# All products of constants taken out of TensorE's stream in a two-block transformer kernel

## The chip, the cores and the metric

The kernel runs on one core of a Trainium2 chip. The metric is the device time of one execution in microseconds (us); lower is better. All times below are from runs on the chip.

## What is computed

The input is a latent sequence of 512 tokens and a context of 256 tokens, both of width 1024, in fp32. Two blocks follow one another.

```python
for layer in range(DEPTH):                       # 2
    sh1, sc1, g1, sh2, sc2, g2 = ada_mod(c[:, None, :], ada_w[layer], ada_b[layer])
    h_lat = rmsnorm(x_lat, norm_mix[layer]) * (1 + sc1) + sh1
    h_ctx = rmsnorm(x_ctx, norm_mix[layer]) * (1 + csc1) + csh1
    if layer % 2 == 0:
        y_ctx, y_lat = hyena_mlstm_mixer(h_ctx, h_lat, ...)
    else:
        y_ctx, y_lat = mla_mixer(h_ctx, h_lat, not last, ...)
    x_lat = x_lat + g1 * y_lat
    x_lat = x_lat + g2 * conv_ffn(rmsnorm(x_lat, norm_ffn[layer]) * (1 + sc2) + sh2, *ffn_p[layer])
...
h = rmsnorm_2(x, norm_mix_w[l])                  # second block, 1 layer
attn = gqa_attention(...)
ssd = bidirectional_ssd(...)
x = x + merged @ w_out[l]
x = x + hierarchical_moe(rmsnorm_2(x, norm_ffn_w[l]), ...)   # 16 experts, 2 per token
```

None of the outputs depends on the products that this document is about.

## The kernel before, in words

The program is a row of stages, each a block in which every engine has its own instruction stream. Streams wait for one another by semaphores. At a block's end stands a barrier for all engines (line 169 in the profile): the next stage begins on every engine when the last one has come to its end. So what a stage costs is set by its slowest engine, and what comes first in a stage can't start before that.

Most of the work is `three_passes` (lines 303 to 305): each fp32 operand is cut into a high and a low part, and TensorE takes three products of them. Weights come by `Stream` (lines 240 to 283): SyncE's queue loads a tile, ScalarE rounds it to the high part (`high`, line 278), VectorE subtracts for the low part (`low`, line 282), and TensorE waits for `ready`. A second load into the same place waits for `low`. At a stage's start TensorE waits for the first tile, unless an earlier stage has fetched it.

Norms have a serial part. In `Norm` ScalarE squares (line 379), VectorE adds the tiles (388), `sum_and_spread` on TensorE sums over partitions (400), ScalarE takes the root (414), VectorE the reciprocal (431) and a diagonal (435), TensorE spreads it (406), and VectorE and ScalarE scale, shift and split tile by tile (441, 421, 425, 448), and TensorE begins its projection with the first tile. `NormOfNorm` (lines 534 to 627) is the same for two norms in one, with 569 and 577 on TensorE. The latent attention's inner norms (lines 640 to 713) have 656 and 663 there.

`keep_running` (lines 286 to 289) issues n products on TensorE of an identity and the constants: 128x128 by 128x256, fp32. They wait for nothing, read tensors that never change, and write a PSUM bank that nobody reads. An fp32 product is two passes in the profile. It stands at 25 places in the source, 37 runs in the executed stream:

- at the start of a stage that waits for weights, 8 products: projections, residual projections, attention inputs (lines 1009, 1341, 1610, 1701, 2413, 2771)
- around the norms: 16 or 20 ahead of the sum, 2 or 6 behind it, 4 or 6 behind the spread (394 to 408, 565 to 579), and 12, 3 and 12 in the latent attention's norms (650 to 666)
- in the recurrent stage (mLSTM): 2, 6 and 3 (1915, 1954, 1960)
- in the state-space stage: 8 ahead of `spread_rows`, 10 ahead of the first unit's product (line 2943), 1 ahead of each of the next five, 16 at the end (2926, 2938, 2963)
- in the router of the experts: 8, 8 and 16 (3440, 3449, 3454)

TensorE's stream is executed in order, so a product of constants delays every real one behind it if that one could already run. The state-space stage on TensorE, where the prediction has a term of its own: `spread_rows(u)` (2903 to 2905) makes a unit's exponents, ScalarE takes the exponential (3010), VectorE multiplies (3081, 3085), and TensorE's 2943 waits for that (`prob`); unit u + 2 is spread ahead of unit u's product. VectorE's `grow` (3046) comes ahead of its first 3081.

## Time and profile before

| | |
|---|---|
| median of 3 runs | 3084.03 us (3082.63 to 3085.0) |
| the profiled execution's own time | 3083.98 us |
| its span, first to last instruction | 3082.2 us |
| busy: TensorE, its weight loads | 2844.0 us, 2309.2 us |
| busy: VectorE, ScalarE, GpSimd | 1721.4 us, 1218.5 us, 181.2 us |
| moved by DMA | 359.71 MB, mean 117 GB/s |

In the profile TensorE is PE (its weight loads PEld), VectorE DVE, ScalarE ACT, GpSimd POOL, SyncE SP. L289 is line 289 of the kernel before. The clock (PEclk) is the share of TensorE's full clock of 2.4 GHz that was granted; it has two levels, 1.00 and 0.50 (1.2 GHz), and a value between them is a mean over a stretch. "idle before" is the time in which the engine had nothing to do just ahead of the instruction, and "<-" names what ended it.

### The profile page before, as it was taken

Reading aid. Unit: us, or ns where it says so; the run is one execution under the profiler, and the core shown is the slowest. Engines: PE = TensorE matmul, PEld = TensorE weight load, DVE = VectorE, ACT = ScalarE, POOL = GpSimd, SP = SyncE. Lnnn points to the kernel's source line nnn. Section 1 sums busy time; section 2 is a strip of 40 time slices with the busy share of each in tenths; the row PEclk is TensorE's granted clock in tenths of the full one; section 3 lists DMA queues with packets and bytes.
Section 4 is the critical chain, followed back from the end, with each engine's and each line's share of the span. In section 5 each row is a group of like instructions: output and inputs, shape, how many; then the busy total and the mean of one; then the engine's idle time right before and its main releaser. Section 6 shows DMA issues by size and latency. Waiting matters only on the chain. (4 is left out here: it accounts for less than half of the span.)

```text
span 3082.2 us, 37662 instructions
## 1 busy us (share of the span) xinstructions
PE 2844.0 (92%) x14114; PEld 2309.2 (75%) x14114; DVE 1721.4 (56%) x2450; ACT 1218.5 (40%) x1621; POOL 181.2 (6%) x160
## 2 busy tenths in 40 slices
PE   7899989799999989998999999989979989899998
PEld 3764877688888888786887887867746667777776
DVE  3764643635767443535854433352258564788887
ACT  4210322324233242433534343244426422577776
POOL 0000001100011000000000000000000000122221
PEclk9989999899999999999999999999988998999999
DMA  5500320021345243202012221312200024799996
GB/s 234 176 21 14 123 96 2 28 93 61 121 141 180 74 150 97 67 25 68 1 49 89 97 95 70 99 55 89 89 8 1 1 70 165 272 364 356 354 356 220
DMA packets 79468, 359.71 MB, mean 117 GB/s; under 512 B 13554, under 2 KB 18451, under 8 KB 54772
## 3 DMA queue, kind: packets, MB, share of 16 engines
q1 hardware_dynamic: 61204, 307.74, 27.9%
q0 software_dynamic: 18144, 50.36, 5.4%
q8 instruction: 76, 1.25, 0.2%
q14 instruction: 44, 0.36, 0.0%
HBM read 356.47 MB, written 16.25 MB: 121 GB/s over the span
## 5 line engine op out<-in xcount | busy, mean ns | idle before, releaser
L303 PE MATMUL ps<-rounded,rounded 128*128 128x512 f32 (+1 forms) x3540 | 1301.8, 368 | 117.9 <-DVEq L1090 20.1
L304 PE MATMUL ps<-rounded,rounded 128*128 128x512 f32 (+1 forms) x3540 | 1281.8, 362 | 0.0
L305 PE MATMUL ps<-rounded,rounded 128*128 128x512 f32 (+1 forms) x3540 | 1280.1, 362 | 0.0
L303 PEld LDWEIGHTS ps<-rounded,rounded 128*128 128x128 f32 x3540 | 677.4, 191 | 240.0 <-issue 76.1
L305 PEld LDWEIGHTS ps<-rounded,rounded 128*128 128x128 f32 x3540 | 676.5, 191 | 102.8
L304 PEld LDWEIGHTS ps<-rounded,rounded 128*128 128x128 f32 x3540 | 678.0, 192 | 96.1
L282 DVE TENSOR_TENSOR rounded<-work,rounded 128x1024 fp32r<-128x1024 f32 (+3 forms) x224 | 306.2, 1369 | 745.0 <-ACT rounded L278 744.7
L278 ACT CAST rounded<-work 128x1024 fp32r<-128x1024 f32 (+3 forms) x224 | 260.5, 1165 | 711.7 <-PE ps L305 614.8
L3716 DVE TENSOR_TENSOR rounded<-work,rounded 128x2048 fp32r<-128x2048 f32 x138 | 309.8, 2285 | 71.6 <-ACT rounded L3536 71.6
L3536 ACT CAST rounded<-work 128x2048 fp32r<-128x2048 f32 x138 | 258.9, 1912 | 74.7 <-PE ps L305 74.7
L289 PE MATMUL ps<-cst 128*128 128x256 f32 x562 | 151.6, 429 | 35.9 <-PEq L169 35.9
L289 PEld LDWEIGHTS ps<-cst 128*128 128x128 f32 x562 | 120.1, 219 | 62.3 <-issue 43.1
L278 ACT ACT_TABLE_LOAD x34 | 43.6, 1283 | 192.4 <-PE ps L305 183.9
L493 DVE SCALAR_TENSOR_TENSOR work<-work,silu_c 128x256 f32<-128x256 f32 x224 | 103.6, 483 | 13.3 <-DMA work<-in_ada_w 7.4
L2283 PE MATMUL ps<-rounded,rounded 128*128 128x256 f32 (+2 forms) x416 | 96.5, 372 | 5.6 <-PEq L169 5.1
L1173 ACT ACTIVATE work<-work 128x768 f32<-128x768 f32 (+1 forms) x44 | 32.5, 739 | 125.3 <-DVE work L1208 125.3
L3414 POOL DMA_INDIRECT out_x<-h,whole x23 | 60.1, 2613 | 349.9 <-ACT h L3578 335.2
L1086 DVE SCALAR_TENSOR_TENSOR work<-ps,vec,work 128x255 f32<-128x255 f32 (+3 forms) x116 | 72.4, 653 | 14.5 <-ACT work L1056 10.6
L2283 PEld LDWEIGHTS ps<-rounded,rounded 128*128 128x128 f32 (+1 forms) x416 | 65.2, 196 | 19.0 <-issue 8.4
L2333 ACT CAST rounded<-ps 128x768 fp32r<-128x768 f32 (+1 forms) x64 | 44.4, 694 | 69.3 <-PE ps L2309 69.2
L1486 PE MATMUL ps<-work 128*128 128x512 f32 x160 | 71.5, 606 | 0.0
L918 DVE SCALAR_TENSOR_TENSOR work<-work,silu_c 128x512 f32<-128x512 f32 x98 | 67.7, 745 | 5.9 <-DMA work<-in_ada_w 4.2
(509 smaller groups left out, 2493.5 us busy)
## 6 DMA issues: line engine op xcount, KB each, us to landing
work<-in_moe SPq DMA_DIRECT2D x138, 1024.0 KB, 8.2
work<-in_ffn_up SPq DMA_DIRECT2D x44, 1024.0 KB, 4.8
work<-in_ada_w POOLq DMA_DIRECT2D x80, 512.0 KB, 4.1
work<-in_ffn_down SPq DMA_DIRECT2D x66, 512.0 KB, 3.4
work<-in_ada_w SPq DMA_DIRECT2D x4, 2048.0 KB, 27.2
work<-in_w_out SPq DMA_DIRECT2D x16, 512.0 KB, 3.5
work<-in_w_gates SPq DMA_DIRECT2D x16, 512.0 KB, 3.5
work<-in_w_in_hy SPq DMA_DIRECT2D x12, 512.0 KB, 4.7
```

What stands on the lines that cost most here:

```text
L278: self.k.nc.scalar.copy(self.parts[s][0], self.raw[s]).then_inc(self.rounded[s], 1)
L282: self.k.nc.vector.tensor_tensor(self.parts[s][1], self.raw[s], self.high_plain[s], ALU.subtract).then_inc(self.ready[s], 1)
L289: k.nc.tensor.matmul(k.bank(bank, 2 * P), k.const("ident"), k.cst[:, 0:2 * P], start=True, stop=True)
L303: k.nc.tensor.matmul(out, sh, mh, start=start, stop=False, **more)
L304: k.nc.tensor.matmul(out, sh, ml, start=False, stop=False, **more)
L305: return k.nc.tensor.matmul(out, sl, mh, start=False, stop=stop, **more)
L493: done = self.k.nc.vector.scalar_tensor_tensor(out=total, in0=tile, scalar=by, in1=total, op0=ALU.mult, op1=ALU.add)
L1086: nc.vector.scalar_tensor_tensor(out=out, in0=k.pair(p)[:, lo + o:hi + o], scalar=k.col(conv_w, n + tiles * (o + taps // 2)), in1=out, op0 ...
L1486: last = nc.tensor.matmul(bank(group, part), tab[part][:, a, n * P:(n + 1) * P], src[:, a, :], start=a == 0, stop=a == count - 1)
L2283: last = nc.tensor.matmul(scores(u)[:, t0 - lo:t0 - lo + n], queries, keys, start=i == 0, stop=i == len(products) - 1)
L3536: nc.scalar.copy(ring.parts[:, c % ring.SPLIT, 0, :], ring.raw[c % ring.RAW]).then_inc(ring.rounded, 1)
L3716: V.tensor_tensor(ring.parts[:, s, 1, :], ring.raw[c % ring.RAW], ring.plain[:, s, 0, :], ALU.subtract).then_inc(ring.ready, 1)
```

## The change

`keep_running` is deleted, with every call of it. Where a norm's `begun` branch or an `elif` held only such a call, the branch goes or is left with its `return`. Nothing else is touched.

```diff
-def keep_running(k, n=8, bank=7):
-
-    for _ in range(n):
-        k.nc.tensor.matmul(k.bank(bank, 2 * P), k.const("ident"), k.cst[:, 0:2 * P], start=True, stop=True)
...
     def sum_and_spread(self, pe):
         k = self.k
         if self.begun:
-            keep_running(k, 6, self.spare)
             return
-        keep_running(k, 16, self.spare)
         pe.wait_ge(self.added, DT - 1)
...
         last.then_inc(self.summed, 1)
-        keep_running(k, 2, self.spare)
         for a in range(self.n):
...
-        keep_running(k, 6, self.spare)
...
         @block.tensor
         def _(pe):
-            keep_running(k, 12, 6)
             done = 0
...
                 last.then_inc(summed, 1)
-            keep_running(k, 3, 6)
...
                 last.then_inc(spread_done, 1)
-            keep_running(k, 12, 6)
...
             if norm:
                 norm.sum_and_spread(pe)
-            elif not stream.ahead:
-                keep_running(k)
...
-            keep_running(k, 8)
             pe.wait_ge(rows_high, 1)
             pe.wait_ge(rows_ready, 1)
             pe.wait_ge(masked, 5)
...
                     widen(u // 2)
-                if u < 6:
-                    keep_running(k, 1 if u else 10)
                 pe.wait_ge(prob, u + 1)
...
             last.then_inc(sum_done, 1)
-            keep_running(k, 16, 2)
```

The other calls go in the same way.

What this does to TensorE's stream is seen at the start of the state-space stage's units, TensorE before (the last exponent row turned, then the first units; "waits" are semaphores):

```order
L289 MATMUL ps<-cst 128x256 x8
L2903 MATMUL ps<-rounded_41984_14620,rounded_50560_14618 128x512 [waits even_33,even_7,even_6]
L2905 MATMUL ps<-rounded_50304_14616,rounded_50560_14618 128x512
L2911 MATMUL ps<-rounded_41984_14620,rounded_38400_14619 128x512
L2912 MATMUL ps<-rounded_42496_14621,rounded_38400_14619 128x512
L289 MATMUL ps<-cst 128x256 x10
L2943 MATMUL ps<-work,h 64x128 [waits even_8,even_12]
L2943 MATMUL ps<-work,h 64x128 x3
L2903 MATMUL ps<-rounded_41984_14620,rounded_50560_14618 128x512 [waits even_11]
L2904 MATMUL ps<-rounded_42496_14621,rounded_50560_14618 128x512
L2905 MATMUL ps<-rounded_50432_14617,rounded_50560_14618 128x512
L289 MATMUL ps<-cst 128x256
```

And the same stretch of the changed kernel, whose line numbers are smaller (L2903 is L2875, L2943 is L2912):

```order
L2868 MATMUL ps<-cst,row 16x128 x3
L2875 MATMUL ps<-rounded_41984_14410,rounded_50560_14408 128x512 [waits even_33,even_7,even_6]
L2877 MATMUL ps<-rounded_50304_14406,rounded_50560_14408 128x512
L2883 MATMUL ps<-rounded_41984_14410,rounded_38400_14409 128x512
L2884 MATMUL ps<-rounded_42496_14411,rounded_38400_14409 128x512
L2912 MATMUL ps<-work,h 64x128 [waits even_8,even_12]
L2912 MATMUL ps<-work,h 64x128 x3
L2875 MATMUL ps<-rounded_41984_14410,rounded_50560_14408 128x512 [waits even_11]
L2876 MATMUL ps<-rounded_42496_14411,rounded_50560_14408 128x512
L2877 MATMUL ps<-rounded_50432_14407,rounded_50560_14408 128x512
```

The runs of L289 are gone, and every wait stands at the instruction where it stood.

## Rows read from the trace of the kernel before

**Rows 1.** The page, part 1: busy time, share of the span, instructions
```profile
PE 2844.0 (92%) x14114; PEld 2309.2 (75%) x14114; DVE 1721.4 (56%) x2450; ACT 1218.5 (40%) x1621; POOL 181.2 (6%) x160
```

**Rows 2.** The page, part 5, products of constants: busy us, mean ns, idle before
```profile
L289 PE MATMUL ps<-cst 128*128 128x256 f32 x562 | 151.6, 429 | 35.9 <-PEq L169 35.9
```

**Rows 3.** Windows behind bare gaps: stretch, length, PE busy (count), PEclk, DMA share, GB/s
```profile
93.55:103.55 10.00, 10.00 (x47) 0.77 0.54 174
...
490.95:500.95 10.00, 10.00 (x50) 0.84 0.01 2
...
2488.20:2498.20 10.00, 10.00 (x31) 0.69 0.32 107
2541.41:2551.41 10.00, 10.00 (x35) 0.79 0.30 105
```

**Rows 4.** Timeline of TensorE: start, us, what, idle before; shortest of those gaps
```profile
490.95 0.40 PE L303 MATMUL ps<-rounded,rounded 128*16 128x256 f32 x1 [3.54 <-DVE rounded L2106]
```

**Rows 5.** Windows behind products of constants, same columns
```profile
607.34:617.34 10.00, 10.00 (x63) 1.00 0.35 105
...
1592.82:1602.82 10.00, 10.00 (x37) 0.83 0.34 106
...
2274.62:2284.62 10.00, 10.00 (x83) 1.00 0.01 2
```

**Rows 6.** Windows of one stage at either clock, TensorE, same columns
```profile
2068.61:2074.50 5.89, 5.89 (x14) 0.50 0.55 178
2076.00:2081.89 5.89, 5.89 (x27) 1.00 0.21 58
```

**Rows 7.** Timeline of TensorE in the norms
```profile
684.89 2.40 PE L400 MATMUL ps<-cst,row 128*128 128x1 f32 x12 [1.84 <-DVE row L388]
...
689.72 2.93 PE L406 MATMUL ps<-h,cst 128*128 128x128 f32 x12 [0.51 <-DVE h L435]
...
1293.33 1.40 PE L400 MATMUL ps<-cst,row 128*128 128x1 f32 x12
...
1295.63 1.60 PE L406 MATMUL ps<-h,cst 128*128 128x128 f32 x12
...
1360.08 2.29 PE L656 MATMUL ps<-cst,h 128*128 128x1 f32 x20
...
1363.61 2.39 PE L663 MATMUL ps<-h,cst 128*128 128x128 f32 x20
...
2047.62 1.95 PE L577 MATMUL ps<-h,cst 128*128 128x128 f32 x16
```

**Rows 8.** Timeline of VectorE in the norm at 1354 to 1373
```profile
1357.98 0.96 DVE L695 TENSOR_TENSOR h<-h 128x768 f32<-128x768 f32 x1 [0.50 <-ACT h L672]
...
1365.08 3.91 DVE L707 SCALAR_TENSOR_TENSOR work<-work,vec,ps 128x512 f32<-128x512 f32 x5
```

**Rows 9.** Timeline of TensorE, the next wait behind the restart at 2052.64
```profile
2068.61 0.79 PE L303 MATMUL ps<-rounded,rounded 128*128 128x512 f32 x1 [4.65 <-DVE rounded L282]
```

**Rows 10.** Timeline of the state-space stage, TensorE and VectorE
```profile
2407.31 0.68 DVE L3058 TENSOR_TENSOR rounded<-ps,rounded 16x512 fp32r<-16x512 f32 x1 [0.84 <-ACT rounded L2991]
...
2411.27 0.49 PE L2903 MATMUL ps<-rounded,rounded 16*128 16x512 f32 x1
...
2413.76 2.98 DVE L3081 TENSOR_TENSOR work<-work 128x512 f32<-128x512 f32 x1 [1.37 <-ACT work L3010]
...
2420.69 1.28 DVE L3081 TENSOR_TENSOR work<-work 128x512 f32<-128x512 f32 x2
2421.65 1.09 PE L2943 MATMUL ps<-work,h 128*64 128x128 f32 x8
...
2423.67 0.59 PE L289 MATMUL ps<-cst 128*128 128x256 f32 x2
```

**Rows 11.** Timeline, work that covers other runs of the products
```profile
2608.85 2.48 DVE L3610 SCALAR_TENSOR_TENSOR h<-h,work 128x1024 f32<-128x1024 f32 x2
...
88.82 1.04 ACT L278 CAST rounded<-work 128x1024 fp32r<-128x1024 f32 x1 [8.48 <-DMA work<-in_w_in_hy]
```

More of the change, by code:

```diff
@@ L564, in sum_and_spread @@
         k = self.k
-        keep_running(k, 20, self.spare)
         pe.wait_ge(self.added, 2 * DT - 2)
@@ L571, in sum_and_spread @@
         last.then_inc(self.summed, 1)
-        keep_running(k, 6, self.spare)
         for n, (spread, diagonal) in enumerate(((self.spread, self.diagonal), (self.first_spread, self.first_diagonal))):
@@ L578, in sum_and_spread @@
                                    start=True, stop=True).then_inc(self.spread_done, 1)
-        keep_running(k, 4, self.spare)
     def shift(self, act):
@@ L1339, in _ @@
         def _(pe):
-            if not stream.ahead:
-                keep_running(k)
             with pe.Fori(0, turns) as i:
@@ L1608, in _ @@
                 norm.sum_and_spread(pe)
-            elif not stream.ahead:
-                keep_running(k)
             def turn(i, first):
@@ L1700, in _ @@
         def _(pe):
-            keep_running(k)
             for j, a in enumerate(token_tiles):
@@ L1914, in _ @@
                 prepare(g)
-            keep_running(k, 2, 2)
             pe.wait_ge(topped, 2)
@@ L1952, in carry @@
                         last.then_inc(state, 1)
-            keep_running(k, 6, 2)
             pe.wait_ge(masked, 3)
@@ L1959, in _ @@
             weigh(0)
-            keep_running(k, 3, 2)
             pe.wait_ge(fade_high, 1)
@@ L2412, in _ @@
         def _(pe):
-            keep_running(k)
             with pe.Fori(0, turns) as i:
@@ L2770, in _ @@
         def _(pe):
-            keep_running(k)
             for j in range(4):
@@ L3439, in _ @@
             pe.wait_ge(tok_kept[0], 4)
-            keep_running(k, 8, 4)
             pe.wait_ge(chosen, 1)
@@ L3448, in _ @@
             last.then_inc(summed, 1)
-            keep_running(k, 8, 4)
             pe.wait_ge(matched, 1)
@@ L3453, in _ @@
             last.then_inc(listed, 1)
-            keep_running(k, 16, 4)
             def turn_seen(t, half):
```

## The prediction, made before the changed kernel was run

> **What bounds the kernel now.** I read the page first: TensorE is busy for 92% of the span [rows 1], so the question at each place is what keeps the other 8%, and what speed TensorE has. The products of constants are 562 passes (281 products, two passes each) with 151.6 us of busy time, and next to them TensorE has 35.9 us of idle time that ends in its own queue, at the barrier between stages [rows 2]. That is 4.9% of the span, but it isn't 4.9% on the path: at most places these products stand in time in which TensorE would wait for something else. So I went through the timeline run by run, in 37 runs, and asked two things of each: did the next real matmul come later than what it waits for, and at which clock did it run.
>
> The clock is the second half. The windows view gives the granted clock in the first 10 us after a restart. Nine restarts come after at least 3.5 us of idle TensorE with no product of constants in the gap; the shortest gap is 3.54 us [rows 4]. All nine run at first at the low level (1.2 GHz): the mean clock over the 10 us is between 0.69 and 0.84, 0.77 over the nine [rows 3]. A clock of 0.77 over 10 us is 2 x 0.23 x 10 = 4.6 us at half speed; the ends are 3.2 and 6.2 us. Twelve restarts come right behind products of constants: nine have 1.00 (2.4 GHz), the first and the last of them shown, and three have 0.83, so 3.4 us at the low level in spite of the products [rows 5]. What low time costs is read in one stage: 14 matmuls pass in 5.89 us at 0.50, 27 at 1.00 [rows 6]; a microsecond at the low level loses 1 - 14/27 = 0.48 us wherever TensorE is the bound.
>
> **The change, part by part.** It removes all 281 products, adds nothing, and moves nothing; no wait, queue or DMA changes.
>
> *Restarts that are fast now.* After the change the stretches ahead of 607.34, 696.98, 1301.57, 1376.35, 1389.26, 1412.04, 1656.48, 2052.64 and 2274.62 are gaps without work on TensorE of 4.3 us or more; ahead of 1656.48 and 2052.64 it is 3.1 us, with only 2 us of passes between that gap and a longer one. By [rows 3, 4] each restarts at the low level for 4.6 us, 4.6 x 0.48 = 2.2 us. Behind eight of them TensorE works almost without a break to the end of its stage, and the barrier there waits for the last matmul's eviction, so the loss is on the path: 8 x 2.2 = 17.6 us. Behind 2052.64 it isn't: TensorE next waits 4.65 us for VectorE [rows 9], which in this stretch works through its own queue, and the loss goes into that wait. Nothing there.
>
> *Restarts that are slow now* (325.37, 452.88, 1592.82): 3.4 us become 4.6, 3 x 1.2 x 0.48 = 1.8 us. The ones at 2488 and 2633 are slow now for as long as any; nothing.
>
> *The norms.* There few small fp32 products are a link of a serial chain. The norm at 684.89 runs at the low level now, the one at 1293 at full speed: L400's twelve passes take 2.40 against 1.40 us, L406's twelve 2.93 against 1.60 [rows 7]. After the change all are slow.
> - At 1293: L406 is waited for by VectorE, 1.3 us more. L400 loses 1.0, but could start 0.9 us earlier; 0.
> - At 1360: L656 waits for VectorE's L695, which ends at 1358.94 [rows 8], and starts at 1360.08, since 12 products of constants stand ahead of it: 1.1 us are given back. Its twenty passes then take 4.0 instead of 2.29, and L663's twenty 4.9 instead of 2.39 [rows 7]. The first part of L663 is hidden by VectorE's L701; the fourth of the five L707 [rows 8] waits for the second part, which ends at about 1368.9 instead of 1366.0, while VectorE would be there at 1367.1. 1.9 us in all.
> - At 2043: sixteen passes of L569 (1.3 us more at L400's rate) and sixteen of L577 (1.95 us now, 1.8 more at L406's rate) [rows 7], 3.1 us.
> - At 685 and 1651 they are slow already; 0.
>
> On L400, L569 and L656, whose moving tile has one column, a rule speaks against a part of this. The Trainium skill, "TensorE: Matmul & The Clock Gate", section "LDWEIGHTS (loading the stationary operand)", gives a weight load's time by its columns alone, with no clock in it. By that these passes would cost the same at either level, the norms 3 us less, and the result would be about 3103. The row of L400 shows 2.40 against 1.40 us for the same twelve passes, and decides.
>
> *The state-space stage at 2406 to 2437*, the one place where the products are plainly late. L2903 waits for L3058, done at 2407.99, and starts at 2411.27, behind eight products. Ten more stand ahead of the first L2943 at 2421.65, though what it waits for, VectorE's first L3081, is done at 2416.74 [rows 10]. Without them that L3081 starts 1.4 us earlier (its idle before) and no more, for VectorE's queue is full ahead of it. The second group of L2943, now at about 2424.2, needs the third L3081's predecessor, one of the pair at 2420.69, which comes 1.0 to 1.4 us earlier: about 2420.4, a gain of 3.8 us. Five single products follow between the next groups, 0.4 us each: 2.0 us. The stage then restarts slow once, 2.2 us. Together 3.6 us less; between 5.8 less and nothing.
>
> *Places I cost at nothing.* At 63.65 six products delay the first matmul, but the stage's next weights land so late that ScalarE's cast at 88.82 ends an idle time of 8.48 us, and TensorE waits for what follows it [rows 11]; should that DMA come early, the price is at most the 2.2 us of a restart. At 2605 eight products end late, but VectorE is in L3610 until 2611.33 and reads the result only then [rows 11]; without that cover it would be a gain of 1.8 us. At 2610, 2621 and 2475 a DMA or VectorE ends later than they do. The eleven products in the recurrent stage (518 to 526) are a few tenths late each and keep the clock for a dense stretch; between 2 less and 2 more, I take 0.
>
> Sum: 17.6 + 1.8 + 1.3 + 1.9 + 3.1 - 3.6 = 22.1 us. The profiled execution took 3083.98 us, which is the median of the runs (3084.03) as well; 3083.98 + 22.1 = 3106.1 us. The ends: with 3.2 us low per restart (1.5 us each) and the norms half hidden, 12.0 + 0.5 + 3.2 - 5.8 + 1.5 = 11.4, so 3095; with 6.2 us (3.0 each), 24 + 4 + 6.3 and no gain at 2406, 34, so 3118.
>
> **The rivals.**
> - *Late waits come free and the clock costs little* (faster). Place: 2406 to 2437 and 1360, 5.8 + 1.1 us, and some tenths at 1283, 1408 and 519: 8 to 10 us less, 3075. For it: the clock falls at three of twelve places in spite of the products [rows 5], so they don't hold it reliably. Against it: nine of nine bare gaps restart low. It decides where the mean low time per restart is below 6.9/(9 x 0.48) = 1.6 us, even with the norms free; no row of [rows 3] is under 3.2.
> - *TensorE isn't the bound behind the restarts.* If in half of the eight stages the rounding by ScalarE and VectorE or a DMA comes last, 8.8 us vanish: 3097. For it: the first pass behind a norm is fed tile by tile at TensorE's own pace. Against it: TensorE has hardly an idle time behind those restarts.
> - *Longer low times.* The clock returns behind dense work; behind 696.98, 1389 and 2420 the work is broken by short waits. At 6.2 us per restart it is 9 x 0.8 = 7 us more: 3113.
> - *It cancels.* Low times near 3.2 us, half hidden, and the whole gain at 2406: within 6 us of now.
>
> **How the numbers follow.** About 0.2% (6.2 us) is what a measurement of this kernel can tell from no change. Forecast 0.55, longer low times 0.12, not the bound 0.14: all three are slower by more than that, 0.81. It cancels: 0.10. Faster: 0.09. The range 3091 to 3119 takes in the first three with the bounds of their costs, and leaves out the faster rival and most of the canceling one, under 0.2.
>
> **What would show it.** After: no row of L289's kind; in the 10 us behind the nine restarts that have 1.00 now, a clock of 0.7 to 0.85; L406 in the norm of 1293 near 2.9 us, L663 near 4.9; the second L2943 group 3 to 4 us closer to its stage's start; TensorE's busy time down by far less than 151.6 us. Each stage from 601 on longer by about 2 us, the one at 2399 shorter by about 3. It is wrong if those clocks stay near 1.00, or if they fall and the stages keep their length.

## The result, and the profile after

| | before | after |
|---|---|---|
| median, runs on the same chip | 3083.38 us (3082.63 to 3085.0, 4 runs) | 3130.49 us (3121.2 to 3133.8, 4 runs) |
| profiled execution, span | 3083.98 us, 3082.2 us | 3132.78 us, 3131.0 us |
| mean granted clock | 0.96 | 0.921 |

The ratio is 1.0151, with a 95% interval of 1.0129 to 1.0174: 47.1 us slower. The forecast was 22.1 us, and the upper end of its range 3119. The direction was right and the size half of what came: three stages, which the forecast had at 1.4 us less together, hold more than half of the loss.

The page's busy line of the kernel after, to be read against [rows 1]:

```profile
span 3131.0 us, 36539 instructions
...
PE 2772.4 (89%) x13552; PEld 2248.6 (72%) x13552; DVE 1721.8 (55%) x2450; ACT 1218.1 (39%) x1621; POOL 183.6 (6%) x160
```

TensorE has 562 passes less, all those of [rows 2], which took 151.6 us of it; its busy time is down by only 71.6 us. The other 80 us are added by its remaining passes, which take longer. The other engines do what they did before.

The windows view of the kernel after shows the first 10 us behind the nine restarts that the forecast named (stretch, length, TensorE busy and count, granted clock, DMA share, GB/s):

```profile
614.69:624.69 10.00, 10.00 (x47) 0.79 0.34 107
706.04:716.04 10.00, 10.00 (x45) 0.75 0.01 2
1314.89:1324.89 10.00, 9.99 (x48) 0.82 0.00 0
1391.67:1401.67 10.00, 10.00 (x33) 0.73 0.14 41
1406.97:1416.97 10.00, 9.95 (x35) 0.83 0.26 79
1430.77:1440.77 10.00, 9.62 (x46) 0.83 0.18 52
1678.57:1688.57 10.00, 10.00 (x34) 0.74 0.00 0
2080.47:2090.47 10.00, 9.99 (x32) 0.70 0.00 0
2303.13:2313.13 10.00, 10.00 (x44) 0.50 0.00 0
```

Eight of the nine have a clock of 0.70 to 0.83, 0.77 in the mean, just the 0.77 of the bare gaps in [rows 3]. The ninth is the surprise: 0.50 through all of its 10 us, with TensorE busy without a break.

Cut at the barriers between the stages, the two traces can be laid side by side. Stage lengths, here and below, come from the one profiled execution of each kernel, medians from all its runs. Three stages hold 26.4 of the 48.8 us by which the profiled executions differ. First the kernel before, whole stages (recurrent, value projection, state space), same columns:

```profile
488.35:601.19 112.84, 91.37 (x548) 0.87 0.01 2
2269.33:2288.06 18.73, 18.02 (x120) 0.92 0.14 32
2399.12:2487.77 88.65, 80.11 (x446) 0.96 0.04 12
```

and the same three stages of the kernel after:

```profile
490.33:608.82 118.49, 93.84 (x526) 0.83 0.01 1
2297.83:2327.46 29.63, 23.72 (x104) 0.50 0.09 20
2438.71:2537.14 98.43, 79.96 (x368) 0.70 0.03 11
```

The recurrent stage is 5.7 us longer, the value projection 10.9, the state space 9.8. For these the forecast had 0, 2.2 and -3.6. In the value projection the 96 passes are the same, and once they have begun TensorE waits for nothing; the lines view of both kernels shows that each takes 1.5 times as long. Before, from the end of the products of constants to the end of the stage (busy us, mean ns):

```profile
L303 PE MATMUL ps<-rounded,rounded 128*128 128x144 f32 x32 | 9.1, 283 | 0.0
```

and after, from the restart to the end of the stage:

```profile
L297 PE MATMUL ps<-rounded,rounded 128*128 128x144 f32 x32 | 13.6, 426 | 11.7 <-DVE rounded L2766 11.7
```

In the state space the low clock begins 6.2 us into the stage and holds for 51.2; a window of just that time:

```profile
2444.92:2496.12 51.20, 47.03 (x131) 0.50 0.00 0
```

What TensorE did in it isn't all narrow. By the lines view of that stretch, of which three rows follow, 72 of the 131 passes have 128 columns, and 43 have 512:

```profile
L2912 PE MATMUL ps<-work,h 128*64 128x128 f32 x72 | 17.7, 428 | 2.4 <-DVE work L3049 2.4
L2877 PE MATMUL ps<-rounded,rounded 128*128 128x512 f32 x11 | 8.8, 796 | 0.0
L2875 PE MATMUL ps<-rounded,rounded 16*128 16x512 f32 x11 | 8.7, 788 | 1.4 <-ACT rounded L2959 1.4
```

In the recurrent stage one stretch of 17.07 us is most of the difference; windows of the kernel before and of the kernel after at the start of the same group of passes:

```profile
523.00:540.00 17.00, 17.00 (x101) 1.00 0.01 1
```

```profile
523.22:540.29 17.07, 15.95 (x49) 0.50 0.01 1
```

So the question for the experiments is not whether the clock is low behind a gap, but why in these three stages it comes back so late, when behind the other eight restarts it is back after 3 to 6 us.

### The profile page after: what moved, and what is told of

Read it like the earlier page. It is cut to its first block and busy times, and to the rows that moved or that the text cites. A ratio compares the mean times of both kernels' runs of the same rounds, so it can differ in the third digit from the quotient of the medians.

```text
span 3131.0 us, 36539 instructions
## 1 busy us (share of the span) xinstructions
PE 2772.4 (89%) x13552; PEld 2248.6 (72%) x13552; DVE 1721.8 (55%) x2450; ACT 1218.1 (39%) x1621; POOL 183.6 (6%) x160
## 5 line engine op out<-in xcount | busy, mean ns | idle before, releaser
L297 PE MATMUL ps<-rounded,rounded 128*128 128x512 f32 (+1 forms) x3540 | 1315.6, 372 | 196.0 <-DVE rounded L282 49.5
L298 PE MATMUL ps<-rounded,rounded 128*128 128x512 f32 (+1 forms) x3540 | 1295.1, 366 | 0.0
L299 PE MATMUL ps<-rounded,rounded 128*128 128x512 f32 (+1 forms) x3540 | 1293.5, 365 | 0.0
L297 PEld LDWEIGHTS ps<-rounded,rounded 128*128 128x128 f32 x3540 | 689.1, 195 | 319.4 <-issue 89.9
L299 PEld LDWEIGHTS ps<-rounded,rounded 128*128 128x128 f32 x3540 | 687.7, 194 | 104.3
L298 PEld LDWEIGHTS ps<-rounded,rounded 128*128 128x128 f32 x3540 | 689.6, 195 | 97.5
L483 DVE SCALAR_TENSOR_TENSOR work<-work,silu_c 128x256 f32<-128x256 f32 x224 | 103.7, 484 | 13.2 <-DMA work<-in_ada_w 7.3
L2257 PEld LDWEIGHTS ps<-rounded,rounded 128*128 128x128 f32 (+1 forms) x416 | 65.2, 196 | 18.9 <-issue 8.1
L2940 POOL TENSOR_TENSOR h<-work,row 128x2048 f32<-128x2048 f32 x2 | 7.9, 3980 | 997.3 <-DVE h L3014 997.3
L2334 DVE TENSOR_REDUCE row<-ps 128x1 f32<-128x768 f32 (+1 forms) x64 | 52.5, 821 | 22.4 <-PE ps L2257 22.2
```

Source lines behind the costliest of these rows:

```text
L297: k.nc.tensor.matmul(out, sh, mh, start=start, stop=False, **more)
L298: k.nc.tensor.matmul(out, sh, ml, start=False, stop=False, **more)
L299: return k.nc.tensor.matmul(out, sl, mh, start=False, stop=stop, **more)
L483: done = self.k.nc.vector.scalar_tensor_tensor(out=total, in0=tile, scalar=by, in1=total, op0=ALU.mult, op1=ALU.add)
L2257: last = nc.tensor.matmul(scores(u)[:, t0 - lo:t0 - lo + n], queries, keys, start=i == 0, stop=i == len(products) - 1)
```

## The experiments

Two theories stood at the outset. **Theory A**: stages made of short passes or of passes with small waits between them (144 columns in the value projection; 128 and 129 columns, mixed with passes of 256 and 512, among the heads of the state space and in the recurrent stage) neither lower a clock that is up nor raise one that is down; what the products of constants did there was to raise it for the whole stage. **Theory B**: after the change low times are longer everywhere, by a general effect of fewer products, and the three stages only show it most. Twelve kernels were run, all in comparison with the kernel before on the same chip. Line numbers are those of the kernel before.

### One stage at a time, and all the others

`e1_no_ss`, the kernel before without the products of the state-space stage (2926, 2938, 2963):

```diff
-            keep_running(k, 8)
...
-                if u < 6:
-                    keep_running(k, 1 if u else 10)
...
-            keep_running(k, 16, 2)
```

> The kernel before with the products of constants of the state-space stage alone taken out (lines 2926, 2938, 2963: 8, 10 + 5, 16). In the changed kernel this stage is 9.8 us longer, with 58 us at the low clock against 7. Theory A (stages of short matmuls can't bring the clock back by themselves, so each such stage loses on its own): the stage 9 to 10 us longer, the whole 3093. Theory B (the forecast's price, 2.2 us per restart, and the long low time there was luck or came in from earlier stages): the stage between 4 us shorter and 2 us longer, the whole 3080 to 3085.

`e2_no_pv`, without those of the value projection (line 2771, `keep_running(k)`):

> The kernel before with the 8 products at the start of the value projection alone taken out (line 2771). In the changed kernel this stage is 10.9 us longer and at the low clock to its end. Theory A: 10 to 11 us longer, the whole 3094, TensorE's matmuls of 144 columns 0.21 us apart throughout. Theory B: 2.2 us, the whole 3086.

`e3_no_ml`, without those of the recurrent stage (1915, 1954, 1960: two, six and three):

> The kernel before with the products of the recurrent stage alone taken out (lines 1915, 1954, 1960: 2, 6, 3). In the changed kernel this stage is 5.7 us longer with 12.7 us more at the low clock. Theory A: 5 to 6 us longer, the whole 3089. Theory B: between 2 less and 2 more.

`e4_only_three`, the changed kernel with the products of just these three stages put back:

> The changed kernel with the products of these three stages put back, so without all the others. Theory A: the other stages lose what the forecast's terms for them give, 22.1 + 3.6 - 2.2 = 23.5 us, or 22.5 by the stages of the changed kernel: the whole 3105 to 3107, and the losses of the four kernels add up to that of the changed one, 47 us. Theory B (low times are longer everywhere): over 30 us here, above 3114, and little in the other three.

| | median us (range) | ratio, 95% interval | more than 3081.09 | own stage |
|---|---|---|---|---|
| before, 13 runs | 3081.09 (3078.94 to 3086.35) | | | |
| e1_no_ss | 3095.25 (3094.58 to 3097.35) | 1.0049, 1.0032 to 1.0065 | 14.2 | +9.9 |
| e2_no_pv | 3097.19 (3088.73 to 3105.02) | 1.0045, 1.0028 to 1.0062 | 16.1 | +11.0 |
| e3_no_ml | 3085.39 (3080.51 to 3094.17) | 1.0014, 1.0004 to 1.0023 | 4.3 | +6.2 |
| e4_only_three | 3094.58 (3093.57 to 3103.55) | 1.0054, 1.0036 to 1.0073 | 13.5 | none of the three |

The last column is from the profiled executions; those of e2 and e3 were the slowest of their runs. Each of the first three kernels loses in its own stage what the changed kernel loses there (9.9, 11.0, 6.2 against 9.8, 10.9, 5.7). The kernels that leave these stages alone show how firm that is: the recurrent stage stays within 0.2 us of its length before and the value projection within 0.4, but the state-space stage is 5.4 us longer in e2, which doesn't touch it, and 3.2 shorter in e4.

By their medians the four add up to 48.1 us, and all taken out together cost 47.1. That they agree so well is partly luck: e1 and e2 lose 4 to 5 us more than their own stages, and e4 missed its expectation, 3094.58 us against 3105 to 3107. In its profile the state space and the attention, from which it takes nothing, are 3.2 and 3.4 us shorter than before. Outside the three stages the changed kernel's profile loses 22.4 us; e4's loses 13.6. In e4, where all the rest is bare, the three are as good as before:

```profile
489.70:602.43 112.73, 91.32 (x548) 0.87 0.01 1
2289.84:2308.89 19.05, 18.33 (x120) 0.89 0.14 32
2415.03:2500.48 85.45, 76.92 (x446) 0.99 0.04 13
```

Theory B falls: it asked for over 30 us in e4 and little in the other three, and the long low times come with the stage's own products taken out, whatever stands elsewhere. The same row for the value projection of e2 is that of the changed kernel once more:

```profile
2278.66:2308.34 29.68, 23.71 (x104) 0.50 0.09 20
```

That other things move a stage's clock too is shown by the state-space stage of the same kernel, with all its products in place, 94.1 us long against 88.7 and with 23 us at the low clock against 7:

```profile
2419.76:2513.84 94.08, 86.09 (x446) 0.88 0.03 12
```

### What raises the clock: other products, and another place

`p1_narrow` gives TensorE something else to do in the same wait:

```diff
-            keep_running(k)
+            for _ in range(28):
+                nc.tensor.matmul(k.bank(7, 2 * P)[:, 0:32], k.const("ident"), k.cst[:, 0:32], start=True, stop=True)
```

> The kernel before, with the eight products of 256 columns at the opening of the value projection stage (line 2771) replaced by 28 products of 32 columns into the same bank: no result changes, and the engine has something to do for about as long. Theory A (the clock of this stage is decided by long dense products ahead of its own products of 144 columns, which by themselves do not raise it): 32 columns count for no more than 144, so the stage stays at the low clock as in the kernel without any products there, 29.6 us against 18.7, and the time is 3092 against 3081 (plus 10.9, perhaps with a random few us in the stages behind). Rival C (anything that occupies the engine over the wait will do): the stage keeps 18.7 us, time 3081 to 3082.

`p2_middle` keeps the eight products and puts them between the second and the third group:

```diff
-            keep_running(k)
             for j in range(4):
+                if j == 2:
+                    keep_running(k)
```

> The kernel before, with the eight products of the value projection stage moved from its opening to the middle, between the second and the third of its four groups of products. Theory A: the first two groups run at the low clock (each 5.3 us longer divided by two, about 5.4 us more than before in all for the pair), the eight products (1.8 us at the low clock, or part of them) turn the clock, and the last two groups run at full speed: stage 18.7 plus 5.4 plus 1 to 2 less the wait that the products no longer share, so 24 to 26 us, time about 3087 to 3088. Rival D (it is the wait at the opening that must be covered, later products come too late, since the engine is by then continuously busy in any case and the clock does not answer): 29.6 us plus 1.8 for the products, time 3093 to 3094.

The kernel before had 3078.25 us on that chip (3072.51 to 3083.85, 19 runs). p1: 3098.76 us, ratio 1.0064 (1.0047 to 1.0081). p2: 3093.0 us, ratio 1.005 (1.0033 to 1.0067). The whole stage of p1, and its narrow products in the timeline (start, us, what, idle before):

```profile
2271.03:2307.38 36.35, 35.63 (x160) 0.50 0.07 17
```

```profile
2271.14 12.13 PE L2772 MATMUL ps<-cst 128*128 128x32 f32 x56 [7.24 <-PEq L169]
```

TensorE is busy for 35.6 of 36.4 us, and the clock is at its lower level in all of them: 12.1 us of passes with 32 columns back to back, and then 24 us with 144, didn't raise it. Rival C, that anything which occupies the engine will do, is out. (The stage lost 17.6 us and not 10.9, since the narrow passes took as long as those of 144 columns at this clock, 12.13/56 = 0.22 us each, and ran 7 us past the arrival of the operands: my expectation had counted a product of 32 columns too cheap.) What it is about the narrow passes that leaves the clock low, no run here separates.

The windows of p2: the wait at the opening, the first two groups, the eight products, the last two groups:

```profile
2269.14:2274.47 5.33, 0.00 (x0) 0.50 0.50 111
2274.47:2286.27 11.80, 11.80 (x53) 0.50 0.01 1
2286.27:2291.14 4.87, 4.87 (x17) 0.68 0.00 0
2291.14:2298.36 7.22, 6.62 (x54) 1.00 0.00 0
```

This is the clearest view of the study. 48 passes of 144 columns take 11.8 us at 0.50, and the other 48, behind sixteen passes of 256 columns, 7.2 us (6.6 busy) at 1.00. The clock rose within those sixteen passes and stayed up behind them through passes that in the first half had not raised it. The loss is as great as without any (10.5 us for the stage) because the products now lie on the path, 4.9 us of it, where I had expected 1 to 2; that they are two passes each, at a clock still half low, was the miss. The median, 3093.0 us, is the one that rival D named; what decides against D is the clock of 1.00 behind the products.

The Trainium skill, "TensorE: Matmul & The Clock Gate", section "Part 1: The HAM clock gate (the "warmup" mystery)", says that the default state is throttled and that activity releases the throttle. By p1 being busy isn't enough: 35.6 microseconds in which the rows show TensorE busy released nothing; in p2 the clock rose within sixteen passes of 256 columns.

### The state-space stage taken apart

`p3_open_out` leaves out the products at the opening and keeps the single ones between the heads and the last sixteen; `p5_singles_out` keeps the opening and leaves out the five singles; `p4_trim` shortens the opening to what the operands need:

p3:

```diff
-            keep_running(k, 8)
...
-                    keep_running(k, 1 if u else 10)
+                    keep_running(k, 1 if u else 0)
```

p4:

```diff
-            keep_running(k, 8)
+            keep_running(k, 3)
...
-                    keep_running(k, 1 if u else 10)
+                    keep_running(k, 1 if u else 4)
```

p5:

```diff
-                    keep_running(k, 1 if u else 10)
+                    keep_running(k, 0 if u else 10)
```

> The kernel before, without the eight and the ten products at the opening of the state-space stage (lines 2926 and 2938), with its five single products (2938) and the sixteen at its end (2963) left in. Where the whole stage lost 9.8 us with all of them out: Theory A1 (the loss arises behind the opening, where the clock falls in the wait and the short products of the heads do not bring it back): at least 7 of the 9.8 us are lost here too, time 3088 to 3091, and the low stretch in the trace begins before the first head. Theory A2 (the single products between the heads, one per head, bring it back or hold it): little is lost, or even won by the late waits (0 to minus 3.6), time 3078 to 3082. In both, the forecast's gain from late waits can show: its terms were 3.8 and 2.0 us for these two places.

> The kernel before, with the openings of the state-space stage cut from eight to three products (line 2926) and from ten to four (line 2938), so that they end when the operands that the next real products wait for are there. If the forecast's term was right that 3.8 and 2.0 us of these products stand behind the arrival of their operands, and if fewer products still keep the clock: 3 to 5 us faster, 3076 to 3078. If the engine's wait is ended by something that comes as late: no change, 3081. If the clock is lost with the fewer products: 3083 to 3091, with a low stretch in the stage.

> The kernel before without the five single products between the heads of the state-space stage (line 2938), with the eight and ten at its opening left in. With the openings out and the singles in, the stage was as long as before, though 24.7 us of it ran at the low clock. Theory A2 (the singles bring the clock back between the heads): here the clock is at its upper level behind the ten, and the question is whether it stays; if the singles are what holds it, the stage loses 2 to 8 us and the low stretch starts within 20 us of the ten products. Theory A3 (once high, the short products and waits of the heads keep it): the stage is as long as before or 1 to 2 us shorter, time within 3 us of the kernel before.

| | median us (range) | before, same chip | ratio, 95% interval | stage, profiled |
|---|---|---|---|---|
| p3_open_out | 3083.99 (3078.61 to 3088.93) | 3078.25 | 1.0022, 1.0011 to 1.0033 | +0.4 us |
| p4_trim | 3077.02 (3073.73 to 3080.13) | 3078.25 | 0.9993, 0.9984 to 1.0003 | -3.1 us |
| p5_singles_out | 3084.76 (3074.37 to 3094.3) | 3082.26 | 1.0013, 0.9999 to 1.0027 | +5.2 us |

First the term whose place the forecast had right. The second group of L2943 in the kernel before (timeline of TensorE; the stage's barrier is at 2399.12, so 25.1 us in):

```profile
2424.19 1.09 PE L2943 MATMUL ps<-work,h 128*64 128x128 f32 x8
```

The first and the second group in p4:

```profile
2419.42 1.84 PE L2943 MATMUL ps<-work,h 128*64 128x128 f32 x8
...
2422.89 1.09 PE L2943 MATMUL ps<-work,h 128*64 128x128 f32 x8
```

and in the kernel after:

```profile
2454.41 1.97 PE L2912 MATMUL ps<-work,h 128*64 128x128 f32 x8
...
2460.68 1.97 PE L2912 MATMUL ps<-work,h 128*64 128x128 f32 x8 [2.43 <-DVE work L3049]
```

With their barriers at 2400.91 and 2438.71 the second groups of both start 22.0 us in, and so does that of p3: 3.1 us earlier than before (forecast 3.8). VectorE sets that time, at either clock.

p4's stage keeps its clock for most of it and is 3.1 us shorter, and in the three kernels below that keep this edit it is 2.2, 3.5 and 3.1 us shorter; over all runs of p4 that doesn't show, since the interval takes in no change. The expected 3 to 5 us were missed. For p3 theory A1 had asked for 7 us lost and A2 for little; the stage says A2, the median lies 5.7 us over the kernel before, so between them (the profiled execution, 3080.57 us, was one of p3's fastest). p3 in three windows, before the fall, in it, behind it:

```profile
2399.65:2405.98 6.33, 5.21 (x44) 1.00 0.00 0
2405.98:2429.87 23.89, 20.69 (x52) 0.50 0.00 1
2429.87:2488.74 58.87, 51.93 (x315) 0.99 0.05 19
```

The low time begins ahead of the first head, as A1 had said, and ends within the heads. The opening gains 3.1 us and the 23.9 us at the low clock give them back. With the singles out as well (e1) the low time is 51.2 us and the stage loses 9.9; the sixteen products that e1 also leaves out stand behind the stage's last real matmul. p5 shows the other side, the clock up for 29.3 us and then down for 23.9:

```profile
2396.85:2426.15 29.30, 26.68 (x141) 1.00 0.00 1
2426.15:2450.04 23.89, 23.89 (x72) 0.50 0.00 0
2450.04:2490.74 40.70, 34.30 (x225) 1.00 0.08 27
```

So theory A has to be corrected in one point. This chain does not reliably hold a clock that is up: here it fell, and TensorE then ran 23.9 us without an idle moment at 0.50 before it rose again. But that the missing singles did it isn't shown. With all products in place the low time was 7.1 us in the profile of the kernel before, 1.5 in e4 and 23.0 in e2, and e2's stage was as long (+5.4) as p5's (+5.2). What stands outside this spread is the 51.2 us at a stretch with every product out, seen twice, in the changed kernel and in e1. How that divides over the opening and the singles is open. That p5 is slower than before is its profiled stage's word; over its runs the interval takes in no change.

### A version with the products where the rows ask for them

`i1_heads`: p4, and products in the stage that turns the heads ahead of the attention, which has none now and in which the clock falls for 30.7 us. `i2_gaps`: besides, products in the longer bare waits, wherever a bank is free. `i3_fewer`: i2 with the misses taken back.

In `heads`, and thus in all three (in i3 with 3, 5 and 4):

```diff
+            pe.wait_ge(rooted, 1)
+            keep_running(k, 3, 0)
             pe.wait_ge(rows_kept, 2)
             pe.wait_ge(inverted, 1)
             for n in range(n_tiles):
+                if n == 4:
+                    keep_running(k, 6, 0)
...
+            keep_running(k, 7, 0)
```

In i2 the rest; i3 leaves out the pair of lines with `summed`:

```diff
@@ ffn_up, end @@
+            if beside:
+                pe.wait_ge(beside.lined, 2 + 8 * DT // beside.UNITS)
+            keep_running(k, 12)
@@ ffn_down, end @@
+            pe.wait_ge(summed, DT * (len(segs) - 1) + 1)
+            keep_running(k, 9, 4 if len(segs) > 1 else 0)
@@ project_residual @@
-                keep_running(k)
+                keep_running(k, 12 if len(segs) == 1 else 8)
@@ project_tokens @@
-            keep_running(k)
+            keep_running(k, 16)
@@ mlstm_core, before the last transposes, and behind them @@
+            keep_running(k, 12, 2)
...
+            keep_running(k, 6)
@@ state_space, end @@
-            keep_running(k, 16, 2)
+            keep_running(k, 24, 2)
@@ merge, end @@
+            keep_running(k, 12)
```

> The trimmed openings of the state-space stage (three and four products), and besides products of constants at three places where the kernel before has none, in the stage that turns the heads of queries and keys ahead of the attention: three before the wait for the inverted roots, six between the fourth and the fifth spread, seven at its end. In the kernel before the clock falls there at 2306.6 and stays low for 30.7 us, 20 of them in the attention behind. Theory A (a chain of short or waiting products does not raise a fallen clock, long dense ones do, and once it is high such a chain keeps it): the clock stays up or comes back before the attention starts, the attention stage (81.8 us) gets 3 to 8 us shorter, 3070 to 3075 for both edits where the kernel before has 3078 to 3081. Rival E (the attention is held by its chain through ScalarE and VectorE, not by TensorE's clock): its stage stays at 81 to 82 us, and the heads' stage gets longer by what the products cost, 3078 to 3081.

> The same, and products of constants in every longer wait that the kernel before leaves bare and where a bank is free: 12 at the end of each feed-forward up stage and of the merge, 9 at the end of each feed-forward down stage, 24 for 16 at the end of the state-space stage, 12 before the last transposes of the recurrent stage and 6 at its end, 16 for 8 at the head of the token projection, 12 for 8 ahead of the latent-only residual projection. Theory A with the forecast's price of 2.2 us for a restart at the low clock: up to ten restarts and the 20 us low stretch of the recurrent stage, 10 to 20 us on top of the one above, 3055 to 3070. Rival F (the stages end so close behind these waits that the products run into the barriers, or their own restart is at the low clock in any case, as at line 289 now): within 3 us of the one above.

> The last version without its nine products at the end of the feed-forward down stages, and with three, five and four products in the stage of the heads. At 1281 those nine kept the clock up, and so the sixteen at the head of the next stage ran at full speed and ended 2 us ahead of the operands they were counted for, and the norm behind them fell to the low clock (stages 1.7 and 3.4 us longer). Theory A, that only the clock of the restart and the end of a product's cover matter: these two stages come back to 71.0 to 71.5 and 65.2 us, the heads' stage stays within 0.5 us of 29.2, all else as in the last version; 5 us faster than that, 3066 to 3071, against 3078 to 3081 of the kernel before. If instead those two stages stay long, the cause is another edit or the phase of the clock, and the time stays at 3073.

| | median us (range) | before, same chip | ratio, 95% interval |
|---|---|---|---|
| i1_heads | 3083.98 (3077.39 to 3090.64) | 3081.17 | 1.0011, 1.0002 to 1.002 |
| i2_gaps | 3073.46 (3065.38 to 3078.89) | 3081.17 | 0.9975, 0.9966 to 0.9984 |
| i3_fewer | 3072.32 (3067.8 to 3076.61) | 3082.26 | 0.997, 0.996 to 0.998 |

i3 beats both kernels: 9.9 us faster than the one before by the medians, and by the two ratios, 0.997/1.0151 = 0.982, about 56 us faster than the changed one. All three missed the times that were expected. i1 was to gain and lost. i2 gained 10.5 us over i1, which rules rival F out, but stayed above 3055 to 3070. i3 was to come to 3066 to 3071 and came to 3072.32. (The profiled executions of i2 and i3 were the fastest of their runs.)

In i1 the heads' stage got 1.2 us longer, the six products ahead of the fifth spread having run at the low clock, and the attention behind it was low for 20 us as before. The windows of the attention stage, first in i2, then in i3, with nearly the same edits ahead of it:

```profile
2318.01:2395.05 77.04, 73.50 (x416) 0.96 0.00 1
```

```profile
2310.07:2394.49 84.42, 80.90 (x416) 0.86 0.00 1
```

and in the kernel before:

```profile
2317.28:2399.12 81.84, 79.14 (x416) 0.88 0.00 1
```

It is 77.0 and 84.4 us long with the same 416 passes, and 81.8 before. p5, e4 and e3, which don't touch it, have 78.4, 78.4 and 84.0. The length goes with the low time, which is 2 x (1 - clock) x length: about 6 us at 77.0, 12 at 78.4, 20 at 81.8, 24 and 25 at 84.4 and 84.0. That is some 0.4 us per low microsecond, so rival E was wrong to say that its clock doesn't matter. My expectation that covering the waits ahead would settle the clock was wrong too: i2 and i3 both cover them. i3's time misses its expectation by less than the 7.4 us by which this stage is longer in its profile than in i2's.

In i2 the sixteen products at the head of the stage at 1281 ran at the full clock and ended 2 us before their operands came, and part of the norm behind them ran at the low clock. Timeline of i2, TensorE, the end of the sixteen and the norm's passes, to be read against the 1.40 us in [rows 7]:

```profile
1281.14 7.14 PE L289 MATMUL ps<-cst 128*128 128x256 f32 x32 [0.73 <-PEq L169]
1290.26 2.00 PE L400 MATMUL ps<-cst,row 128*128 128x1 f32 x12 [1.97 <-DVE row L388]
```

Its stage from 1281.03 on was 73.2 us long. Without the nine products that i2 has ahead of it, it is 71.0 in i3 (71.5 before), as expected. The one at 2030 came back from 68.7 to 64.9 (65.2 before), but this doesn't show that the nine are the cause: e2, which has none of them and whose edit lies behind this stage, is 3.5 us longer there too, its products having ended 2 us early in the same way. Where i3 gained, in its profile against that of the kernel before: 3.1 us in the state space, 2.9 and 2.0 in the two stages behind it, 2.2 and 1.9 in the feed-forward down stages, 1.3 and 1.2 at the token and the residual projection; it lost 2.6 us in the attention. In the recurrent stage low time went from 28.6 to 13.7 us and the stage stayed as long (112.7 against 112.8 us). Most of the time at the low clock that went away stood around a wait for VectorE, in the kernel before:

```profile
591.08 2.82 PE L1991 MATMUL ps<-cst,work 128*128 128x128 f32 x12 [7.09 <-DVE work L2214]
```

The same is seen in e1 and p5, where nothing there was changed and the low time was 20.5 and 20.9 us at the same length. Low time that doesn't lie on the path costs nothing; the 17.07 us in the middle of the stage cost about 6.

## Why the prediction was right in direction and half in size

Against the profiled execution, stage by stage from barrier to barrier:

| step of the forecast | forecast | measured |
|---|---|---|
| restarts at 607, 697, 1376, 1389, 1412, 1656 | 6 x 2.2 = 13.2 | 1.4, 2.2, 2.4, 1.4, 1.0, 2.1 = 10.5 |
| stage of 1301 (restart and norm) | 2.2 + 1.3 | 3.4 |
| norm at 1360 | 1.9 | 0.4 |
| stage of 2043 (norm; its restart at 0) | 3.1 | 1.8 |
| restarts slow before: 325, 453, 1593 | 1.8 | 0.6 + 0.5 + 0.7 = 1.8 |
| restart at 2275, value projection | 2.2 | 10.9 |
| state space | -3.6 | 9.8 |
| recurrent stage | 0 | 5.7 |
| places at nothing, and the rest | 0 | about 4.6 |

**Right.** That the products' 151.6 us are mostly in waits; that bare gaps restart at the low clock, and by how much (0.77 forecast, 0.77 measured on eight); about the price of 0.48 us per low microsecond (in the value projection the stretch behind the restart took 24.33 us against 13.44, 0.45). The three slow ones came to the forecast 1.8 us; with terms of 0.5 to 0.7 us each, which is less than stages move between kernels that don't touch them, that is luck. The norms' passes slowed as foreseen, those of L406 at 1307 to 2.93 us, and the twenty of L656 and of L663, with the gap between their two rows:

```profile
1372.47 1.28 PE L642 MATMUL ps<-cst,h 128*128 128x1 f32 x8 [3.85 <-DVE h L679]
1373.93 2.72 PE L642 MATMUL ps<-cst,h 128*128 128x1 f32 x12 [0.17 <-DVE h L679]
1377.73 4.64 PE L648 MATMUL ps<-h,cst 128*128 128x128 f32 x20 [1.08 <-DVE h L685]
```

4.0 and 4.6 us, where 4.0 and 4.9 stood. The passes with one column took 1.7 and 1.9 times as long (4.00 against 2.29 us for twenty, 2.72 against 1.40 for twelve at 1304), which is against the rule of the Trainium skill that gives a weight load by its columns alone ("TensorE: Matmul & The Clock Gate", "LDWEIGHTS (loading the stationary operand)"). The loads themselves show it: those of L289 in the kernel before took 0.19 us at the upper level and 0.33 at the lower (medians of 447 and 115). The stage lost only 0.4 us instead of 1.9, because the first passes could start 2.8 us behind the barrier instead of 5.3: the products had stood in front of all of them, tile by tile, and I had counted 1.1 us for that.

**Wrong, one step for three stages.** "By [rows 3, 4] each restarts at the low level for 4.6 us" took a mean over nine bare gaps for a property of the gap. All nine are followed by dense passes, nearly all of 256 and 512 columns, behind which the clock was back after 3 to 6 us; where something else follows a gap, the low time lasted longer. In the value projection passes of 144 columns follow, and the low time lasted to the end of the stage: 24.3 us from the restart, where the term had 4.6. The state space was written down as "then restarts slow once, 2.2 us", over a chain of heads in which passes of 128 columns alternate with wider ones; it was low for 58 of its 98 us in the profile. The sum there was 3.1 us gained at the place foreseen and, to make up the 9.8, 12.9 lost, not 2.2. The recurrent stage I held at "0, between 2 less and 2 more"; I had written that its products "keep the clock for a dense stretch" and gave no price to what happens when they don't, 17.07 us at 0.50. The misses are 8.7, 13.4 and 5.7 us, 27.8 in all; with them the sum of 22.1 becomes 49.9, and the profiled executions differ by 48.8. That it comes so close is helped by two rests that nearly cancel: the other restarts and norms came 5.6 us below their terms, and places at nothing 4.6 above.

Rows that could have told were in view. In [rows 5] the value projection had 1.00 with 83 passes in 10 us, nearly all of 144 columns, and I counted it among twelve alike. And "nine of nine" was not the whole count: the kernel before has four more restarts behind a bare gap of 3.5 us or more, at 198.80, 591.08, 2227.49 and 2255.82. All four are low at first, so the rule of the restart stands, but one of them doesn't come back within its 10 us:

```profile
591.08:601.08 10.00, 5.62 (x24) 0.50 0.00 0
```

It stands at the end of the recurrent stage, where 24 passes of 128 columns with waits between them follow the gap. That was a low time of at least 10 us where the forecast's range for a restart ended at 6.2.

The rival of longer low times named the right mechanism ("the clock returns behind dense work") but at the wrong places and at 6.2 us per restart, again the largest value among dense ones. "Late waits come free" came about at its place and was outweighed; "TensorE isn't the bound" and "it cancels" didn't happen.

**Open.** What sets the low time of the attention stage, and with it its length between 77 and 84 us, and why the clock stays low through the state space's passes of 512 columns. Stages that were not touched moved by 1 to 5 us between kernels (the one at 401 by 2.3 to 3.1 us in eight of the thirteen, the last one by 3.9 to 4.0 in five), so terms under 2 us in a single trace are not shown by it, and in the state space and the attention not even larger ones. "About 4.6" in the table is such a rest and isn't attributed; half of it is the stage at 401. Which of the eleven products in the recurrent stage hold its clock wasn't tried.

## What to carry to other kernels

A gap on TensorE doesn't cost a fixed restart; look at what follows it, and take the price from a row in which the same passes follow. Ahead of the three stages here in which the clock was slow to come back, products of constants in the waits that are there anyway were worth about 6 to 11 microseconds each; ahead of dense passes of 256 and 512 columns they were worth one to two and a half. They should end when the operands arrive. Count them at the clock that they will really run at, and look first whether the stage's end hangs on TensorE at all.

## What the runs showed of the hardware that was not expected

- The level of the clock depends on what ran before, not only on what runs: 48 passes of 144 columns ran at 0.50 for 11.8 us, and 48 more of the same kind, behind sixteen passes of 256 columns, at 1.00 (p2_middle). TensorE busy for 35.6 of 36.4 us without a rise is the longest case (p1_narrow).
- Passes of 512 columns don't always bring it back: 51.20 us at 0.50 with TensorE busy for 47.03 and 43 of its 131 passes of 512 columns (the changed kernel's state space; e1_no_ss has the same 51.2 us).
- At the low clock a pass with 32 columns takes as long as one with 144: 56 in 12.13 us, 0.22 us each (p1_narrow).
- Keeping the clock up ahead of a stage can slow it: products counted for the low clock ended 2 us early at the full one, and part of the norm behind them was slow (i2_gaps, 73.2 us against 71.0 in i3_fewer).
